# Making the first projections of a layer during the last expert periods of the layer ahead

## The chip, the cores and the metric

The kernel runs on one core of a Trainium2 chip. The metric is the device time of one execution in microseconds. The profile is of one execution of the same program, and its times below count from the first instruction of that execution.

## The reference, cut to what matters

Two blocks of two layers each run one after the other on 256 latent tokens, with 256 context tokens beside them, all in float32. A layer is a mixer followed by an expert stage:

```
xl = norm(hl) * (1 + scale) + shift          # latent tokens
xc = the same for the context tokens
y  = mixer(xl, xc) @ w_out;  hl += gate * y
hl += gate * experts(hl)                     # per token 8 heads x 16 experts of 16384
```

The mixers are: layer 0, a recurrent cell beside a differential attention; layer 1, windowed attention with key and value heads shared (16 query heads, 4 key and value heads); layer 2, attention through a latent vector (`zq` 384 wide, `zkv` 320 wide, both projections of the normalized tile); layer 3, pooling on latent tokens alone. From layer 1 on the context tokens only give keys and values. In layer 1 their projection is `kv` (512 wide: 256 of keys, 256 of values); in layer 2 it is `zkv` (256 that are normalized, 64 that hold the rotary part), and the context is an input of its own, `ctx_2`.

The expert stage projects a token to 16 vectors of 128, scores each against 128 keys, picks 16 experts for a head, gathers the two rows `u` and `v` of each (1024 float32 each), and sums `gate * gelu(u.x) * v`.

## The kernel before, in words

Tokens lie in four tiles of 128 partitions: tiles 0 and 1 are context (`CTX`), 2 and 3 latent (`LAT`). `H` holds the residual stream. The work of each engine is written out by hand, in order, with three step counters (one for each of TensorE, VectorE and ScalarE) on which the others wait.

A layer's **front** is its input and first projections. `front_input(t)` transposes the normalized tile `xn(l, t)` (8 transposes of 128x128), ScalarE or VectorE copy it from PSUM to `xT`, and `natural(l, name, (t,), ...)` multiplies it by a weight block (8 products of 128x128 by the block's width; each is two matmul instructions in the trace, a transposition is one). In layer 1 the front's order on TensorE is: `kv` of tiles 0 and 1, then for tiles 2 and 3 `kv`, `q0`, `q1`. In layer 2: `zkv` of tiles 0 and 1, then `zkv`, `zq` of tiles 2 and 3. In layer 3: `in0`, `in1` of tiles 2 and 3. Between them stand `take_beside()` calls, each one block of the modulation product for the next layer (2 MB of weights, 16 matmul instructions; every fourth also adds a bias, line 588, and ScalarE then copies and stores the group, `take_mods`). The rest of the twelve blocks stand in the attention loop, at the steps in `MODS_L1` (35 steps in layer 1).

Weights come in blocks, issued in a fixed order by SyncE (`block_list`, line 439) into five slots: 0 and 1 of a weight ring, `x0`, `x1` (which lies over two slots of the experts' ring) and `gates`. An issue waits until the slot's last block is used up, and the blocks behind it wait with it. `q0`, `zq`, `in1` and blocks in `x1` also wait for the sum of the third-last expert of the layer ahead.

An **expert period** (a unit) is 16 experts of one head for one tile. `POOL` issues a gather of 128 rows of 8 KB (1 MB) for each (line 494) into a ring of 8 slots, VectorE makes the dot product (line 2056), ScalarE the weight and a diagonal matrix (lines 1282 to 1286), TensorE the sum in PSUM (line 1007, two products 512 wide, four matmul instructions in the trace), and that sum frees the slot for the gather eight further on. Layer 0 has 32 periods, the others 16. Beside the 16 experts of a period, at the places in `PE_BESIDE` and `ACT_BESIDE`, stand the query products and scores of the period three ahead (`query`, `take`), and on VectorE the top-k of the period two ahead. In the last 16 periods, here called tail 0 to tail 15, no query is left for tails 13 to 15 and no top-k for tails 14 and 15. VectorE puts the context's normalized tiles in `H` (`next_context`) by tail 5, and from tail 12 on the norm of tile 2 and its next input (`end_of_layer(l, 2)`); that of tile 3 comes after the last sum.

## Time and profile before

| | |
|---|---|
| median of 3 runs | 4391.81 us (4379.93 to 4396.69) |
| the profiled execution | 4388.36 us, span 4386.6 us |
| TensorE busy | 3685.0 us (84%), mean granted clock 0.955 |
| VectorE busy | 2780.4 us (63%) |
| ScalarE busy | 1619.3 us (37%) |
| GpSimd busy | 1404.8 us (32%) |
| DMA | 1569.57 MB, mean 358 GB/s, 75.7% of it the experts' gathers |

The busy shares are means over stages with different limits. The expert stages run from 507 to 1827 us (layer 0), 2084 to 2723 (layer 1), 3006 to 3612 (layer 2) and 3777 to the end (layer 3); between them lie the mixers.

### The profile page before, as it was taken

What the parts mean: (1) busy time and instruction counts of PE and PEld (TensorE: products, weight loads), DVE (VectorE), ACT (ScalarE), POOL (GpSimd) and SP (SyncE); (2) the same over time, 40 slices, a digit from 0 to 9 for tenths busy, and PEclk for the clock granted to TensorE, in tenths of its full rate; (3) what the DMA queues carried; (4) which work ended last, traced back from release to release, by engine and by line L of the source; (5) the groups of instructions that cost most, each with busy time, mean ns of one, the idle gap of its engine ahead of it and who ended that gap; (6) DMA issues with size and microseconds to landing.
All of it is one profiled execution on the core that took longest, in us unless ns stands there. A gap on an engine that the chain in (4) does not pass through costs nothing.

```text
span 4386.6 us, 42868 instructions
## 1 busy us (share of the span) xinstructions
PE 3685.0 (84%) x11886; PEld 1734.8 (40%) x11886; DVE 2780.4 (63%) x7000; ACT 1619.3 (37%) x4854; POOL 1404.8 (32%) x1337
## 2 busy tenths in 40 slices
PE   5997988888888888898888888888888878888886
PEld 2444433344333333355333333453333324333332
DVE  3227766677776677446766675357667755766775
ACT  0123234444444344232444443124444431444443
POOL 0000243444443444201444442014434431434342
PEclk7988999999999999998999999999999999999999
DMA  6335699999999999863999999649999995999997
GB/s 248 135 136 202 262 421 421 421 419 413 413 419 419 416 414 407 330 274 146 421 421 421 420 410 374 238 183 421 421 421 420 411 390 207 411 421 421 421 411 333
DMA packets 207216, 1569.57 MB, mean 358 GB/s; under 512 B 23072, under 2 KB 23200, under 8 KB 30592
## 3 DMA queue, kind: packets, MB, share of 16 engines
q0 software_dynamic: 191952, 1370.57, 75.7%
q1 hardware_dynamic: 14832, 196.06, 11.4%
q8 instruction: 94, 1.54, 0.1%
q14 instruction: 146, 1.20, 0.1%
q10 hardware_dynamic: 192, 0.20, 0.0%
HBM read 1565.50 MB, written 1.25 MB: 357 GB/s over the span
## 4 chain that ended last, share of the span: by engine, by line
DMA 47%; PE 26%; DVE 9%; ACT 5%; issue 3%; DVEq 1%; POOL 1%; ACTq 0%; POOLq 0%
DMA arena<-uv,idx 46%; PE banks L1007 13%; PE banks L547 5%; DVE arena L2056 5%; PE banks L665 2%; ACT diag L1286 1%; PE banks L580 1%; ACT wgt L1284 1%; ACT gel L1282 1%; ACT L1282 1%; ACT L1070 1%; PE banks L840 1%; DMA weight_ring<-weights 1%; PE banks L561 1%; POOL arena L494 1%
## 5 line engine op out<-in xcount | busy, mean ns | idle before, releaser
L1007 PE MATMUL banks<-arena,diag 128*128 128x512 f32 x5120 | 2514.6, 627 | 547.7 <-ACT diag L1286 542.6
L494 POOL DMA_INDIRECT arena<-uv,idx x1280 | 1375.6, 1075 | 2313.3 <-PE banks L1007 1799.0
L2056 DVE CUSTOM_DVE_ANT_0 arena<-arena 128x1024 f32<-128x1024 f32 x1280 | 1566.8, 1225 | 854.0 <-DMA arena<-uv,idx 836.4
L1007 PEld LDWEIGHTS banks<-arena,diag 128*128 128x128 f32 x5120 | 926.7, 196 | 1982.2 <-ACT diag L1286 1205.8
L1282 ACT ACTIVATE gel<-dot 128x1 f32<-128x1 f32 x1280 | 258.5, 202 | 1674.1 <-DVE dot L2056 1672.7
L1286 ACT ACTIVATE diag<-consts_sb,wgt 128x128 f32<-128x128 f32 x1280 | 514.0, 402 | 92.2 <-issue 5.2
L1284 ACT ACTIVATE wgt<-gel,gate 128x1 f32<-128x1 f32 x1280 | 376.8, 294 | 90.4 <-issue 3.2
L547 PE MATMUL banks<-weight_ring,arena 128*128 128x512 f32 (+2 forms) x876 | 369.2, 580 | 5.3 <-DVE hidden_sb L1565 1.8
L547 PEld LDWEIGHTS banks<-weight_ring,arena 128*128 128x128 f32 x876 | 165.6, 191 | 198.4 <-issue 185.9
L471 POOL DMA_DIRECT2D row_ring<-mods x34 | 18.6, 556 | 598.3 <-DMA mods<-diag 256.2
L665 PEld LDWEIGHTS banks<-arena,weight_ring 128*128 128x128 f32 x1408 | 170.3, 192 | 39.7 <-issue 39.5
L665 PE MATMUL banks<-arena,weight_ring 128*128 128x128 f32 x1408 | 170.7, 275 | 0.0
L665 PEld LDWEIGHTS banks<-arena 128*128 128x128 f32 x1152 | 143.8, 199 | 31.3 <-issue 28.5
L665 PE MATMUL banks<-arena 128*128 128x128 f32 x1152 | 144.9, 282 | 3.3 <-ACT arena L1042 1.7
L580 PE MATMUL banks<-weight_ring,silu_cond 128*32 128x512 f32 x640 | 91.8, 699 | 37.7 <-DMA weight_ring<-weights 37.7
L1042 ACT COPY arena<-banks 128x512 f32<-128x512 f32 (+1 forms) x49 | 26.4, 573 | 223.0 <-PE banks L645 120.6
L2056 DVE DVE_READ_ACCUMULATOR2_ANT dot<- 128x1 f32 x1280 | 105.8, 83 | 0.0
L1282 ACT ACT_TABLE_LOAD x76 | 97.5, 1283 | 1.3
L1070 ACT ACT_TABLE_LOAD x73 | 93.7, 1283 | 1.3
L1536 DVE COPY arena<-banks 128x512 f32<-128x512 f32 (+3 forms) x43 | 25.5, 619 | 78.3 <-PE banks L533 58.1
L675 PEld LDWEIGHTS banks<-arena 128*128 128x128 f32 x320 | 48.9, 194 | 51.5 <-issue 31.2
L1561 DVE TENSOR_TENSOR arena<-banks,row_ring 128x512 f32<-128x512 f32 (+1 forms) x30 | 25.9, 864 | 68.2 <-PE banks L547 55.6
(252 smaller groups left out, 2353.2 us busy)
## 6 DMA issues: line engine op xcount, KB each, us to landing
weight_ring<-weights SPq DMA_DIRECT2D x67, 2048.0 KB, 7.9
arena<-weights SPq DMA_DIRECT2D x18, 2048.0 KB, 11.5
arena<-uv,idx POOLq DMA_INDIRECT x1280
row_ring<-mods POOLq DMA_DIRECT2D x34, 512.0 KB, 14.1
row_ring<-gains POOLq DMA_DIRECT2D x18, 512.0 KB, 13.8
arena<-keys SPq DMA_DIRECT2D x4, 1024.0 KB, 13.6
weight_ring<-weights SPq DMA_DIRECT2D x2, 1536.0 KB, 14.7
arena<-weights SPq DMA_DIRECT2D x3, 1024.0 KB, 9.9
```

What stands on the lines that cost most here:

```text
L494: pool.indirect_dma_start(out=ring[:, RING_SLOT[k], :], out_offset=None, in_=A[f"uv{l}"], in_offset=bass.IndirectOffsetOnAxis(ap=idx[:, UN ...
L547: ins = mm_(bank[:, b, 0:c1 - c0], src(kk, t), w[:, kk, c0:c1], start=kk == 0, stop=kk == k - 1)
L561: ins = mm_(bank[:, b, 0:ncols], w[:, kk, c * P:(c + 1) * P], src(kk), start=kk == 0, stop=kk == k - 1)
L580: ins = mm_(bank[32 * j:32 * j + 32, 7, :], cond, w[:, k2, j * 512:(j + 1) * 512], start=q == 0 and k2 == 0, stop=False, skip_group_check= ...
L665: ins = mm_(bank[:, b, 0:P], w[:, kk, c * P:(c + 1) * P], xT2[:, kk, i * P:(i + 1) * P], start=kk == 0, stop=kk == KC - 1)
L675: ins = mm_(bank[:, b, q * P:(q + 1) * P], qT[:, 2 * m + q, :], keys_sb[:, 2 * h + q, :], start=True, stop=True)
L1007: ins = mm_(bank[:, yb, :], diag[:, s, :], ring[:, s, D + hf * 512:D + hf * 512 + 512], start=first, stop=last, skip_group_check=True)
L1070: AF(ex[:, :], cv[:, :], ACT.Exp, bias=neg[:, :], accum_out=es[:, :]).then_inc(sems["act"], done("act", ("exps", *u)))
L1282: AF(gel[:, s:s + 1], dot[:, s:s + 1], ACT.Gelu)
L1284: AF(wgt[:, s:s + 1], gel[:, s:s + 1], ACT.Copy, scale=gate[:, n, j:j + 1])
L1286: AF(diag[:, s, :], ident, ACT.Copy, scale=wgt[:, s:s + 1]).then_inc(sems["act"], done("act", ("diag", k)))
L2056: sig(V.tensor_tensor_reduce(out=ring[:, s, 0:D], in0=ring[:, s, 0:D], in1=xnat_of(u[0], u[1]), scale=1.0, scalar=0.0, op0=ALU.mult, op1=A ...
```

## The change

The context's projections of layers 1 and 2 and the first product of tile 2 in layers 1, 2 and 3 are made during the last seven expert periods of the layer ahead. A one-tile buffer in a part of `XNAT` that is free then holds the transposed input. The context results are kept in `H[:, t, 0:512]`, from where the attention reads them; layer 2's norm of the context latents moves with them (`context_latents`).

```
+XAHEAD = (None, XNAT + D, XNAT + 2 * D, XNAT + 2 * D)
+AHEAD_NAME = (None, "kv", "zkv", "in0")
-PE_BESIDE = {0: (2, 5, 8, 12, 13), None: (2, 7, 11, 13, 14)}
-ACT_BESIDE = {0: (3, 6, 9, 13, 14), None: (4, 9, 12, 13, 15)}
+PE_BESIDE = {0: (2, 5, 8, 12, 13), None: (2, 6, 9, 12, 14)}
+ACT_BESIDE = {0: (3, 6, 9, 13, 14), None: (4, 8, 10, 13, 15)}
-    out += block("x0", 1, "kv") + block(0, 1, "q0") + mods(2, 0, 1) + block("x1", 1, "q1")
+    out += block("x0", 1, "kv") + block(0, 1, "q0") + block("x1", 1, "q1") + mods(2, 0, 1)
-MODS_L1 = (1, 4, 8, 12, 16, 20)
+MODS_L1 = (0, 2, 5, 8, 11, 14, 17, 20)
...
 # GpSimd: the load of ctx2 into H waits longer
-                    pool.wait_ge(*after("mm", 1, "xT", 1, 1))
+                    pool.wait_ge(*after("mm", 1, "O", 31))
...
 # TensorE, front of layer 1
-                    for t in CTX:
-                        front_input(t)
-                    for t in CTX:
-                        front_ready(t)
-                        natural(1, "kv", (t,), xs, KC, 512, last=False)
+                    for name in ("q0", "q1"):
+                        natural(1, name, LAT[:1], xs, KC, 512, last=False)
                     take_beside()
-                    for t in LAT:
-                        front_input(t)
-                    for t in LAT:
-                        front_ready(t)
-                        natural(1, "kv", (t,), xs, KC, 512, last=t == 3)
-                        if t == 3:
-                            take_beside()
-                        for name in ("q0", "q1"):
-                            natural(1, name, (t,), xs, KC, 512, last=t == 3)
-                            take_beside()
+                    front_input(3)
+                    front_ready(3)
+                    for name in ("kv", "q0", "q1"):
+                        natural(1, name, LAT[1:], xs, KC, 512)
+                        take_beside()
...
 # TensorE, front of layer 2
+                    natural(2, "zq", LAT[:1], xs, KC, 384, last=False)
                     take_beside()
+                    front_input(3)
+                    front_ready(3)
+                    natural(2, "zkv", LAT[1:], xs, KC, 320)
+                    natural(2, "zq", LAT[1:], xs, KC, 384)
+                    for _ in range(4):
+                        take_beside()
...
 # TensorE, front of layer 3
+                    natural(3, "in1", LAT[:1], xs, KC, 512, last=False)
+                    front_input(3)
+                    front_ready(3)
+                    for j in range(2):
+                        natural(3, f"in{j}", LAT[1:], xs, KC, 512)
...
 # TensorE, beside the experts (ScalarE has the copies in the same places)
+                def ahead_input(m, t):
+                    pe.wait_ge(*after("xn", m, t))
+                    for half in range(2):
+                        b = new_bank(m, "xT", t, half)
+                        for k in range(4):
+                            ins = nc.tensor.transpose(...)
+                        ins.then_inc(sems["pe"], done("pe", ("mm", m, "xT", t, half)))
+                        yield
+                def ahead_product(m, t):
+                    name = AHEAD_NAME[m]
+                    width = 320 if m == 2 else 512
+                    n, w = weights((m, name), KC)
+                    pe.wait_ge(*after("ev", m, "xT", t, 0))
+                    pe.wait_ge(*after("ev", m, "xT", t, 1))
+                    b = new_bank(m, name, t, 0)
+                    for kk in range(KC):
+                        ins = mm_(bank[:, b, 0:width], xahead(m)[:, kk, :], w[:, kk, :], ...)
+                        if kk == 3:
+                            yield
+                    ins.then_inc(sems["pe"], done("pe", ("mm", m, name, t, 0)))
+                    yield
...
+                    tail = n - len(units) + 16
+                    if l < 2 and 9 <= tail <= 12:
+                        t = (tail - 9) // 2
+                        beside = chain(beside, ahead_input(l + 1, t) if tail % 2 else ahead_product(l + 1, t))
+                    if l < 3 and tail == 14:
+                        beside = chain(wait_turns(3), ahead_input(l + 1, 2))
+                    if l < 3 and tail == 15:
+                        beside = ahead_product(l + 1, 2)
...
 # ScalarE, layer 1: the group of modulations moves behind the copies of v; layer 3: a wait for the last sum
-                    for t in tiles:
-                        if t == 3:
-                            take_mods(6)
+                    for t in LAT:
...
+                    take_mods(6)
...
 # VectorE, in tails 12 to 15 of layer 1
+            def context_latents():
+                _, mg = row(2, "mlag", 0)
+                for t in CTX:
+                    c = H[:, t, 0:256]
+                    dve.wait_ge(*after("ev", 2, "zkv", t, 0))
+                    V.tensor_copy(H[:, t, 320:384], H[:, t, 256:320])
+                    V.tensor_copy(H[:, t, 384:448], H[:, t, 256:320])
+                    sig(dve.drain(), ("kr", t))
+                    squares(c, H[:, t, 512:768], small[:, 32 + t:33 + t])
+                    yield
+                    rsqrt(small[:, 32 + t:33 + t], 1.0 / 256, EPS)
+                    yield
+                    dve.drain()
+                    sig(V.scalar_tensor_tensor(out=c, in0=c, scalar=small[:, 32 + t:33 + t], in1=mg[:, 384:640], ...), ("zkv_n", t))
+                    yield
```

## Rows read from the trace of the kernel before

**Rows 1.** The page's part 4: the chain that ended last, share by engine.

```profile
DMA 47%; PE 26%; DVE 9%; ACT 5%; issue 3%; DVEq 1%; POOL 1%; ACTq 0%; POOLq 0%
```

**Rows 2.** Windows of 5 us: width, busy (count) by engine, clock, DMA share, GB/s.

```profile
1685.00:1690.00 5.00, 4.77 (x23) 3.03 (x23) 4.62 (x12) 2.44 (x9) 3.61 (x2) 1.00 0.90 339
1690.00:1695.00 5.00, 5.00 (x13) 2.28 (x12) 4.47 (x10) 2.13 (x8) 2.83 (x2) 1.00 1.00 367
1695.00:1700.00 5.00, 3.97 (x13) 1.73 (x12) 3.30 (x11) 1.84 (x6) 3.32 (x4) 1.00 0.95 336
...
1790.00:1795.00 5.00, 4.00 (x9) 1.38 (x9) 2.46 (x4) 1.80 (x6) 1.91 (x3) 1.00 1.01 421
```

**Rows 3.** Timeline of TensorE about the end of layer 0's experts.

```profile
1672.73 1.95 PE L665 MATMUL banks<-arena,weight_ring 128*128 128x128 f32 x16
...
1824.69 1.98 PE L1007 MATMUL banks<-arena,diag 128*128 128x512 f32 x4 [0.47 <-ACT diag L1286]
...
1830.28 13.90 PE L547 MATMUL banks<-arena 128*128 128x512 f32 x32
```

**Rows 4.** The chain in order of time, layer 1's front: start, us, what.

```profile
1863.72 7.44 DMA weight_ring<-weights
...
1873.18 7.78 DMA weight_ring<-weights
...
1899.79 1.85 PE banks L580 x16
...
1905.19 1.18 PE banks L820 x4
```

**Rows 5.** Timeline of SyncE: weight issues at the end of layers 0, 1, 2.

```profile
1821.84 0.80 SPq L439 DMA_DIRECT2D weight_ring<-weights  x2
...
2718.08 0.33 SPq L439 DMA_DIRECT2D weight_ring<-weights  x1
...
3607.48 0.33 SPq L439 DMA_DIRECT2D weight_ring<-weights  x1
```

**Rows 6.** The page's part 6: median us from issue to landing.

```profile
weight_ring<-weights SPq DMA_DIRECT2D x67, 2048.0 KB, 7.9
```

**Rows 7.** Timeline of VectorE: last step of tile 3's input, layers 1, 2, 3.

```profile
1835.06 1.23 DVE L1419 TENSOR_TENSOR arena<-arena,row_ring 128x1024 f32<-128x1024 f32 x1
...
2732.84 1.23 DVE L1419 TENSOR_TENSOR arena<-arena,row_ring 128x1024 f32<-128x1024 f32 x1
...
3624.50 1.23 DVE L1419 TENSOR_TENSOR arena<-arena,row_ring 128x1024 f32<-128x1024 f32 x1
```

**Rows 8.** Windows as in 2: the attention loop of layer 1.

```profile
1905.20:2003.60 98.40, 90.48 (x625) 64.64 (x626) 55.56 (x194) 49.79 (x133) 0.00 (x0) 0.84 0.42 168
```

**Rows 9.** Timeline of TensorE, layer 2's front.

```profile
2725.63 8.85 PE L547 MATMUL banks<-weight_ring,arena 128*128 128x320 f32 x32 [0.96 <-DVE hidden_sb L1567]
...
2749.62 9.73 PE L547 MATMUL banks<-weight_ring,arena 128*128 128x320 f32 x32
...
2768.98 3.64 PE L580 MATMUL banks<-weight_ring,silu_cond 128*32 128x512 f32 x16 [5.04 <-DMA weight_ring<-weights]
...
2774.95 1.92 PE L580 MATMUL banks<-arena,silu_cond 128*32 128x512 f32 x16 [0.81 <-ACT diag L1053]
```

**Rows 10.** Timeline of TensorE, layer 3's front.

```profile
3615.03 13.97 PE L547 MATMUL banks<-weight_ring,arena 128*128 128x512 f32 x32 [1.83 <-DVE hidden_sb L1565]
3628.84 1.04 PE L533 MATMUL banks<-consts_sb,arena 128*128 128x128 f32 x8
3630.71 13.97 PE L547 MATMUL banks<-weight_ring,arena 128*128 128x512 f32 x32 [0.83 <-ACT arena L1042]
```

**Rows 11.** The chain in order of time, last period of layer 0's experts.

```profile
1787.27 15.24 DMA arena<-uv,idx
```

**Rows 12.** Windows of 2 us, as in 2, in layer 1's attention loop.

```profile
1962.00:1964.00 2.00, 1.05 (x4) 0.23 (x4) 1.70 (x7) 0.71 (x2) 0.00 (x0) 1.00 0.98 410
...
1966.00:1968.00 2.00, 2.00 (x12) 2.00 (x12) 0.32 (x2) 1.45 (x4) 0.00 (x0) 0.50 1.12 474
```

More of the change, by code:

```diff
@@ L394, in program, with xahead, wait_turns @@
         xT2 = v3(XT2, KC, 2 * P)
+        def xahead(l):
+            return v3(XAHEAD[l], KC, P)
+        def wait_turns(n):
+            for _ in range(n):
+                yield
         qT = v3(QT, 4, P)
@@ L1105, in _ @@
                 if l < 3:
-                    for t in tiles:
-                        front_input(t, 2 if l and t < 3 else 1)
+                    for t in tiles if l == 0 else (3,):
+                        front_input(t, 1)
                 if l == 2:
@@ L1286, in expert_weight, with ahead_input, ahead_product @@
                     AF(diag[:, s, :], ident, ACT.Copy, scale=wgt[:, s:s + 1]).then_inc(sems["act"], done("act", ("diag", k)))
+                def ahead_input(m, t):
+                    for half in range(2):
+                        copy_T((m, "xT"), t, xahead(m)[:, 4 * half:4 * half + 4, :], half)
+                        yield
+                def ahead_product(m, t):
+                    yield
+                    b = b_(m, AHEAD_NAME[m], t, 0)
+                    c = 320 if m == 2 else 512
+                    ev(a.copy(H[:, t, 0:c], bank[:, b, 0:c]), m, AHEAD_NAME[m], t, 0)
+                    yield
                 units = units_of(l)
@@ L1299, in _ @@
                         beside = take(units[n + 3])
+                    tail = n - len(units) + 16
+                    if l < 2 and 9 <= tail <= 12:
+                        t = (tail - 9) // 2
+                        beside = chain(beside, ahead_input(l + 1, t) if tail % 2 else ahead_product(l + 1, t))
+                    if l < 3 and tail == 14:
+                        beside = chain(wait_turns(3), ahead_input(l + 1, 2))
                     if n == 0:
@@ L2112, in _ @@
                     run(beside)
-                    if (n in (10, 13) and l == 0) or n == len(units) - 11 or tail == 14:
+                    if (n in (10, 13) and l == 0) or n == len(units) - 11 or tail == (15 if l == 1 else 14):
                         run(between)
```

65 lines of the change are left out of this document (29 added, 36 removed).

## The prediction

> **What bounds the kernel now.** I read the chain that ended last first. It goes through DMA for 47% of the span and through TensorE for 26% [rows 1], so there is no single limit: the next thing to read is which stage has which. In windows of 5 us a quiet stretch of an expert stage moves 421 GB/s with the DMA engines full [rows 2], the most that any expert window shows. A gather is 1.049 MB, so a period of 16 needs 39.9 us of DMA. TensorE's part of the same period comes from its timeline: 32 matmul instructions 512 wide took 13.90 us, 0.434 each [rows 3], so the 64 of a period's sums take 27.8 us and its query products about 4.4 us (two groups of 1.95 and some 0.5 for the scores) [rows 3]: 32.2 us. The ring is thus bound by DMA with 7.7 us of TensorE to spare in a period, 12.1 where no query is left. The fronts are the opposite. After the last sum (end 1826.7) TensorE works almost without a break to the last modulation block before layer 1's attention (1901.6) [rows 3, 4]. There the bound is TensorE with short waits for weights: the two DMA pieces of the chain, 7.44 and 7.78 us, lie mostly behind a product, since a block is issued only when the last one in its slot is used up [rows 4]. So the change takes work from where TensorE is the bound to where DMA is. What it is worth must be read from each front.
>
> **Layer 1's front.** It loses the transpositions of tiles 0, 1 and 2 (1.04 each [rows 10]), the `kv` product of those three tiles (6.95 each [rows 3]) and two of six modulation blocks (1.85 each [rows 4]). Laid out anew: `q0` is issued at 1821.84 [rows 5] and with the median landing of 7.9 [rows 6] is there at 1829.7. `q0` and `q1` of tile 2 take 13.9, to 1843.6 (`q1`, issued right behind and moved ahead of the modulation block, lands about 5 us after `q0`, in time). Then one block (1.85): 1845.5. Tile 3's input was ready at 1836.3 [rows 7], so it does not hold. Transposition 1.04 and 0.83 until it is copied [rows 10]: 1847.4. Then `kv` 6.95, block 1.85, `q0` 6.95, block, `q1` 6.95, block: 1873.8. The blocks all lie in slot 1, each issued when the last is used up; 7.8 to land [rows 4] against a product of 6.95 that covers it leaves about 0.9 a block, twice: 1875.6, and 0.9 for the bias: 1876.5. Before it was 1901.6, so 25.1 us less. Two things take some back. ScalarE now copies and stores the modulation group (some 1.8 us) just before its six copies of the transposed keys and queries, on which the first scores wait: 1.4. And two more blocks stand in the attention loop, 3.7 us; TensorE is busy 90.5 of 98.4 us there [rows 8], so little of it is free, but the one at step 0 stands where the loop fills: 3.0. Bounds for these two together: 0 (both in gaps) to 5.5. **Layer 1: 20.7 us less.** The later load of `ctx2` costs nothing: nothing but the gathers, which wait longer anyway, stands behind it on GpSimd, and VectorE asks for it a period later. The context copies in the attention are read from `H` instead, at no price.
>
> **Layer 2's front.** It loses `zkv` of tiles 0 to 2 (32 instructions for two tiles took 8.85, so 4.4 a tile [rows 9]), three transpositions, and on VectorE two of six norms. But tile 3's input is ready only at 2734.1 [rows 7], and the work that covered that wait is gone. `zq` is issued at 2718.1 [rows 5], 1.5 MB, there by about 2725; 5.3 us (the rest of 9.7 for `zkv` and `zq` together [rows 9]), a block to about 2732.4, then TensorE waits to 2734.1, 1.04 and 0.83 more, and 9.7 for tile 3: about 2746. `zkv`'s slot is then free at 2740.6 instead of 2754.2, 13 to 14 us earlier, and behind it the blocks come one after another as they did: in the trace the fourth starts at 2768.98 after 5.04 idle, and the fifth ends at 2776.9 [rows 9]. All of that chain of landings moves with the slot. The fourth block took 3.64 instead of 1.9, and was held by the load of the fifth, issued with it; now that one is issued 2 us behind. I take 15 (bounds 12 and 18). **Layer 2: 15 us less.**
>
> **Layer 3's front.** `in1` is issued at 3607.5 [rows 5], there at 3615.4; 7.0 us to 3622.4. Tile 3's input is ready at 3625.7 [rows 7]: with the product gone TensorE now waits 3.3 us. Then 1.04, 0.83 and the two products 13.97: 3641.6 instead of 3644.7 [rows 10]. **Layer 3: 3 us less.** Of 8 us that it gives away, 5 are lost to VectorE's chain. The wait that ScalarE gets here is for a sum long made.
>
> **The expert periods.** Added on TensorE in the layers 0 and 1: in tails 9 to 12, twice 1.04 and 6.95 (layer 0: 16.0 us), twice 1.04 and 4.4 (layer 1: 10.9); in tails 14 and 15 8.0, 5.4 and 8.0 us in layers 0, 1, 2. Together 48.3 us. The cover is the ring: eight gathers are 19.9 us of DMA, and of that a gather spends 15.24 between issue and landing [rows 11], of which 2.5 are its own transfer: the rest, some 12 us less what a lone gather needs to start, it waits behind others, and the engines may be late by that before DMA runs dry. A half product (3.5 us) between two sums fits, and is made good at 0.75 us an expert. In tails 14 and 15 nothing else competes: nothing. In tails 9 to 12 it is not so clean. There the ring already ran dry once: 339, 367 and 336 GB/s in three windows of tail 12 [rows 2] lose 2.6 us, where VectorE has the top-k, the residual and the norm of tile 2, and TensorE then worked through its backlog (5.00 of 5). A half product put behind such a backlog costs up to its length. ScalarE, too, waits at expert 15 for the second half product before it can copy it, and with it the next period's first weight. Bounds: 0, and 26.9 if all of tails 9 to 12 shows. Only tail 12 of two layers is near dry, and about one half product in each (3.5 and 2.2) falls there: **5 us more**. VectorE's norm of the context latents (two times about 4 us) lies in tails 13 to 15 of layer 1, where it is idle half of the time: nothing. With that cover gone it would be 8. The moved places of the queries change nothing that I can find: each still has ScalarE's copy two experts before its use.
>
> **Sum.** 20.7 + 15 + 3 - 5 = 33.7 us less than the profiled execution's 4388.4: 4354.7. That execution was 3.4 under the median of the runs, so I say **4358**.
>
> **The clock.** In layer 1's attention the granted clock fell from 1.00 to 0.50, that is from 2.4 to 1.2 GHz, after TensorE had been busy only 1.05 of 2 us [rows 12], and the loop's mean is 0.84 [rows 8]. The new waits in the fronts of layers 2 and 3 are of that size. The price from rows: the products behind a fall run at half speed, as the fourth block of layer 2 did (3.64 for 1.92 [rows 9]); if it takes half of layer 3's two products and of layer 2's 9.7, that is 12 us more. If on the other hand the denser blocks keep the loop of layer 1 at full clock, its 16 points of clock on 98.4 us are worth up to 15, say 10. The Trainium skill, in "TensorE: Matmul & The Clock Gate", section "What's actually happening", states that the throttled state is the default and that activity releases it; by that rule the new waits speak against this change, and the sum would be 12 us worse. The trace has waits of 1.8 us at both fronts (layers 1 and 3) with the clock kept, so I leave it out of the sum.
>
> **Rivals and chances.**
> 1. My forecast, 4348 to 4368: 0.55.
> 2. The ring has no room in tails 9 to 12: all 26.9 shows instead of 5, 4380. For it: the dry windows [rows 2]. Against it: 7.7 us spare in each period. 0.13.
> 3. The products are not hidden at all, tails 14 and 15 included: 48.3 for nothing against 38.7 gained, 4401, slower than before. It decides at 38.7 us lost of 48.3; beyond that the ring at a half clock would be needed for over 0.5%. Against it: in the last period TensorE is busy 4.0 of 5 us [rows 2]. 0.04.
> 4. The clock falls in the new waits (12 more): 4370. 0.12.
> 5. The clock holds in layer 1's loop (10 less): 4348 or under. 0.08.
> 6. The weights bound the fronts: with the cover gone, each block of modulation waits for its landing in full, some 8 us more in layer 1 and 6 in layer 2: 4372. 0.08.
>
> The 80% range takes in cases 4, 5 and 6 and most of 2: 4340 to 4378. A measurement of this kernel can tell about 0.5% (22 us) from no change, so faster means under 4370: most of case 1, all of 5, half of 4 and a third of 6. That is 0.74; slower by over 0.5% is 0.03; the rest 0.23.
>
> **What would show it.** In the profile after: `kv`, `zkv` and `in0` products beside sums at line 1007 of tails 10, 12 and 15; layer 1's attention starting about 24 us sooner after the last sum than the 78.5 us of before (1826.7 to 1905.2 [rows 3, 4]); in layer 2 the first `uqn` product about 15 sooner; in layer 3 only 3 sooner, with an idle TensorE that waits for VectorE; expert stages of layers 0 and 1 a few us longer, of layer 2 equal. The forecast is wrong if the windows of tails 9 to 12 show DMA well under 421 GB/s for more than 5 us a layer, or the clock is near 0.5 in the new fronts.

## The result, and the profile after

| | before | after |
|---|---|---|
| median of the runs | 4389.59 us (4 runs, 4379.93 to 4396.69) | 4344.36 us (4 runs, 4342.51 to 4351.19) |
| ratio of the runs | | 0.9904, 95% interval 0.9891 to 0.9917 |
| the profiled execution | 4388.36 us | 4343.52 us |
| TensorE busy, mean clock | 3685.0 us, 0.955 | 3659.4 us, 0.958 |

By the ratio the change made the kernel 42 us faster (36 to 48 by the interval), 1.0% of its time; 34 were forecast. 4344 lies within the stated range of 4340 to 4378, but below the 4348 to 4368 of the forecast's own case, where rival 5 had its place. Two pairs of profiles of the same two programs give the stages. For each stage the table has the time between two products of TensorE: from the first to the last sum of an expert stage, from there to the next layer's first product behind its front (the scores in layer 1, `uqn` in layer 2, the pooling in layer 3), through layer 1's attention loop, and the rest of the mixer.

| us | before | before, again | after | after, again | forecast |
|---|---|---|---|---|---|
| start to first sum | 506.8 | 519.4 | 512.6 | 512.9 | 0 |
| experts 0 | 1319.9 | 1319.8 | 1319.5 | 1319.3 | } |
| experts 1 | 660.5 | 660.5 | 661.8 | 661.8 | } +5 |
| experts 2 | 662.2 | 662.0 | 662.7 | 662.2 | } |
| experts 3 | 654.1 | 653.1 | 653.9 | 653.7 | 0 |
| front of layer 1 | 78.5 | 78.7 | 54.5 | 57.2 | -23.7 |
| its attention loop | 96.4 | 96.3 | 90.6 | 88.4 | +3.0 |
| its rest | 60.9 | 60.8 | 58.4 | 60.0 | 0 |
| front of layer 2 | 58.1 | 57.9 | 42.4 | 46.9 | -15 |
| its rest | 169.0 | 169.1 | 168.5 | 168.8 | 0 |
| front of layer 3 | 33.3 | 33.3 | 30.3 | 33.4 | -3 |
| its rest | 72.7 | 72.7 | 72.6 | 72.7 | 0 |
| first sum to last sum | 3865.6 | 3864.3 | 3815.3 | 3824.4 | -33.7 |

The first row is untouched by the change and yet varies by 12.6 us from one execution to the next, about as much as the whole times of before's two profiles differ (11.3), which is why I read effects of a few us from the stages.

Two figures given ahead of the prediction are to be read otherwise. By the first sum the expert stages of before start at 506.8, 2062.4, 2950.1 and 3718.3 us (the later ones not at 2084, 3006 and 3777). And 75.7% is the share of the 16 DMA engines' time that the gathers' queue took; of the bytes it moved 1371 of 1570 MB, 87%. The loop of before ends at 2001.6, so the window of [rows 8] and the loop lengths in the expectations (98.4, 92.7) count some 2 us of what follows it.

The page's part 4 of after, against [rows 1]: three points of the chain have gone from DMA to TensorE and ScalarE.

```profile
DMA 44%; PE 28%; DVE 9%; ACT 6%; issue 3%; DVEq 1%; POOL 1%; ACTq 0%; POOLq 0%; SPq 0%
```

The timeline of TensorE in after, last period of layer 0's experts and on into layer 1's front (start, us, what, and in brackets the idle time before and what ended it). Line 1008 is the sum, line 1032 the new product, in two halves, line 557 `natural`:

```profile
1797.89 1.98 PE L1008 MATMUL banks<-arena,diag 128*128 128x512 f32 x4 [0.50 <-ACT diag L1323]
1799.71 3.60 PE L1032 MATMUL banks<-arena 128*128 128x512 f32 x8
1803.14 7.03 PE L1008 MATMUL banks<-arena,diag 128*128 128x512 f32 x16
1810.01 3.60 PE L1032 MATMUL banks<-arena 128*128 128x512 f32 x8
1813.44 8.80 PE L1008 MATMUL banks<-arena,diag 128*128 128x512 f32 x20
1822.74 1.98 PE L1008 MATMUL banks<-arena,diag 128*128 128x512 f32 x4 [0.50 <-ACT diag L1323]
...
1830.12 1.98 PE L1008 MATMUL banks<-arena,diag 128*128 128x512 f32 x4 [0.47 <-ACT diag L1323]
```

This is the whole mechanism in a few lines. A sum (four instructions, 1.98) is normally followed by 0.5 us of idleness. After each half product of 3.60 TensorE runs sums back to back: four, then five. By 1822.74 the 0.5 us gap is back, so the delay is paid off, and the last sum is on time. DMA stayed full meanwhile. Windows of after in the same columns as [rows 2]. The first two lie just behind the products of tail 10, the next two in tail 12, with its top-k and the norm of tile 2, the two after them where tail 13 begins:

```profile
1630.00:1635.00 5.00, 5.00 (x13) 2.06 (x12) 3.21 (x9) 1.73 (x6) 0.80 (x1) 1.00 0.99 360
1635.00:1640.00 5.00, 5.00 (x14) 2.20 (x12) 4.36 (x16) 2.33 (x9) 3.26 (x3) 1.00 0.92 329
...
1695.00:1700.00 5.00, 5.00 (x15) 2.33 (x14) 4.60 (x10) 1.77 (x7) 1.87 (x2) 1.00 0.86 323
1700.00:1705.00 5.00, 5.00 (x16) 2.34 (x15) 3.65 (x10) 2.77 (x10) 3.01 (x3) 1.00 0.99 375
...
1715.00:1720.00 5.00, 5.00 (x12) 2.01 (x11) 4.44 (x16) 3.59 (x13) 1.89 (x2) 1.00 0.94 383
1720.00:1725.00 5.00, 5.00 (x13) 2.26 (x12) 4.56 (x15) 1.96 (x7) 3.44 (x4) 1.00 0.93 341
...
1800.00:1805.00 5.00, 5.00 (x13) 2.23 (x12) 2.47 (x4) 1.83 (x7) 0.94 (x1) 1.00 1.01 421
```

In tail 12 the rates 323, 375 and then 406 cost DMA 1.9 us, where the 339, 367 and 336 of before [rows 2] cost 2.6: the new pieces did not deepen that dip, which stands where VectorE is busiest (up to 4.6 of 5 us). But there is a new one. From 1630 to 1645, right behind the two halves of tail 10 (they start at 1622.56 and 1629.43), the rates are 360, 329 and 365, which cost 2.5 us; before has 419 to 424 there. In the second execution of after it comes again (354 and 338 from 1632.3 to 1642.3), and the one of tail 12 does not. Over tails 9 to 12 of layer 0 (four windows of 39.87 us, counted back from the last sum) DMA loses 5.3 and 3.3 us against 421 GB/s in after's two executions and 4.5 in both of before, so what the new pieces take in one place is made up in another, and the stage is not longer.

The chain of after through layer 1's front, in order of time, as in [rows 4]:

```profile
1827.28 7.69 DMA weight_ring<-weights
...
1861.74 7.97 DMA weight_ring<-weights
```

`q0` landed 2.9 us after the last sum ended (1832.1), and two blocks of modulation idled TensorE for 1.01 and 0.81, the rest of their 7.97 and 7.77 us of landing lying behind a product.

The timeline of TensorE in after, fronts of layers 2 and 3, as in [rows 9, 10]; the last sums ended at 2697.5 and 3571.1:

```profile
2699.17 5.43 PE L557 MATMUL banks<-weight_ring,arena 128*128 128x384 f32 x16 [1.70 <-DMA weight_ring<-weights]
...
2708.30 1.09 PE L543 MATMUL banks<-consts_sb,arena 128*128 128x128 f32 x8 [1.85 <-DVE arena L1476]
2710.23 9.71 PE L557 MATMUL banks<-weight_ring,arena 128*128 128x320 f32 x32 [0.83 <-ACT arena L1078]
...
2728.86 3.27 PE L590 MATMUL banks<-weight_ring,silu_cond 128*32 128x512 f32 x16 [3.60 <-DMA weight_ring<-weights]
...
3573.92 8.83 PE L557 MATMUL banks<-weight_ring,arena 128*128 128x512 f32 x16 [2.85 <-DMA weight_ring<-weights]
3584.50 1.09 PE L543 MATMUL banks<-consts_sb,arena 128*128 128x128 f32 x8 [1.76 <-DVE arena L1476]
3586.43 13.97 PE L557 MATMUL banks<-weight_ring,arena 128*128 128x512 f32 x32 [0.83 <-ACT arena L1078]
```

Both fronts now wait for VectorE (line 1476, the last step of tile 3's input, line 1419 before) where a product stood. In layer 3 the clock had already fallen once, behind the wait of 2.85 us: the windows from 3574 to 3578 have it at 0.68 and 0.50, and `in1` took 8.83 us, where it took 7.13 in the second execution behind a wait of 3.01. It cost nothing there, since the product ends ahead of VectorE all the same. And the loop of layer 1, with the stretch in which its clock is down, against [rows 8]:

```profile
1945.00:1950.00 5.00, 3.18 (x24) 2.31 (x23) 3.19 (x11) 2.74 (x9) 0.00 (x0) 1.00 0.94 384
1950.00:1955.00 5.00, 5.00 (x20) 3.47 (x19) 2.32 (x9) 2.60 (x8) 0.00 (x0) 0.50 0.99 424
1955.00:1960.00 5.00, 4.73 (x30) 3.74 (x28) 3.34 (x12) 2.51 (x6) 0.00 (x0) 0.82 0.50 208
...
1886.60:1977.20 90.60, 81.33 (x642) 55.17 (x643) 54.05 (x189) 48.92 (x131) 0.53 (x1) 0.96 0.59 239
```

The mean clock rose from 0.84 to 0.96. This is the one place where the sign of a term was wrong.

### The profile page after: what moved, and what is told of

Same layout as the page of the kernel before. It is cut to its first block, busy times and chain, and to the rows that moved or that the text cites. A ratio compares the mean times of both kernels' runs of the same rounds, so it can differ in the third digit from the quotient of the medians.

```text
span 4341.7 us, 42866 instructions
## 1 busy us (share of the span) xinstructions
PE 3659.4 (84%) x11886; PEld 1730.5 (40%) x11886; DVE 2777.5 (64%) x6996; ACT 1620.4 (37%) x4856; POOL 1442.2 (33%) x1337
## 4 chain that ended last, share of the span: by engine, by line
DMA 44%; PE 28%; DVE 9%; ACT 6%; issue 3%; DVEq 1%; POOL 1%; ACTq 0%; POOLq 0%; SPq 0%
DMA arena<-uv,idx 43%; PE banks L1008 16%; DVE arena L2126 4%; PE banks L557 4%; PE banks L675 2%; ACT diag L1323 1%; DMA weight_ring<-weights 1%; PE banks L590 1%; ACT wgt L1321 1%; ACT L1319 1%; ACT L1106 1%; POOL arena L504 1%; ACT gel L1319 1%; PE banks L847 1%; PE banks L571 1%
## 5 line engine op out<-in xcount | busy, mean ns | idle before, releaser
L504 POOL DMA_INDIRECT arena<-uv,idx x1280 | 1413.1, 1104 | 2167.9 <-PE banks L1008 1761.8
L557 PE MATMUL banks<-weight_ring,arena 128*128 128x512 f32 (+2 forms) x812 | 350.6, 591 | 10.8 <-DMA weight_ring<-weights 7.5
L557 PEld LDWEIGHTS banks<-weight_ring,arena 128*128 128x128 f32 x812 | 153.8, 191 | 198.7 <-issue 178.8
L675 PEld LDWEIGHTS banks<-arena,weight_ring 128*128 128x128 f32 x1408 | 171.5, 193 | 40.2 <-issue 39.9
L675 PE MATMUL banks<-arena,weight_ring 128*128 128x128 f32 x1408 | 171.8, 276 | 0.0
```

The costliest lines, as they stand in the source:

```text
L504: pool.indirect_dma_start(out=ring[:, RING_SLOT[k], :], out_offset=None, in_=A[f"uv{l}"], in_offset=bass.IndirectOffsetOnAxis(ap=idx[:, UN ...
L557: ins = mm_(bank[:, b, 0:c1 - c0], src(kk, t), w[:, kk, c0:c1], start=kk == 0, stop=kk == k - 1)
L675: ins = mm_(bank[:, b, 0:P], w[:, kk, c * P:(c + 1) * P], xT2[:, kk, i * P:(i + 1) * P], start=kk == 0, stop=kk == KC - 1)
```

## The experiments

### Both kernels once more

The same programs, profiled again.

> The kernel before, unchanged, for a second profile. Two theories of why layer 1's attention loop took 98.4 us before and 92.7 after, though two modulation blocks more stand in it: (a) each execution differs in how long the clock stays at half speed after ScalarE's copy and store of the last modulation group (32 us before, 8 us after), so a second profile of the same kernel may give anything from 88 to 98 us for the loop; (b) the order of the blocks before decides it, so this profile shows the long stretch at half clock and 97 to 99 us again. The time as before, 4380 to 4397.

> The kernel after, unchanged, for a second profile and a tighter ratio: 0.989 to 0.991. (a) the loop of layer 1 takes anything from 90 to 100 us; (b) 92 to 93.5 us again, with the half clock for less than 12 us. The expert stages last as long as before within 2 us each under both.

Before: 4399.69 us (one run). After: 4351.53 us median, ratio 0.9909 (0.9882 to 0.9937). In before, the loop and its half clock came again as (b) had it; in after the loop took 88.4 us and had no half clock at all, which is outside (b) (90 to 91.5 us by this count). Before repeats to 0.2 us in all three fronts and in the loop; after does not: its fronts took 57.2, 46.9 and 33.4 us instead of 54.5, 42.4 and 30.3. TensorE's timeline of the second execution of after, at the first product of layer 1's front and in the fronts of layers 2 and 3:

```profile
1835.33 10.04 PE L557 MATMUL banks<-weight_ring,arena 128*128 128x512 f32 x16 [3.05 <-DMA weight_ring<-weights]
...
2710.47 1.09 PE L543 MATMUL banks<-consts_sb,arena 128*128 128x128 f32 x8 [1.88 <-DVE arena L1476]
2712.39 12.70 PE L557 MATMUL banks<-weight_ring,arena 128*128 128x320 f32 x32 [0.83 <-ACT arena L1078]
...
3590.98 1.09 PE L543 MATMUL banks<-consts_sb,arena 128*128 128x128 f32 x8 [3.30 <-DVE arena L1476]
3592.91 17.04 PE L557 MATMUL banks<-weight_ring,arena 128*128 128x512 f32 x32 [0.83 <-ACT arena L1078]
```

and windows of 2 us of the same execution:

```profile
3588.00:3590.00 2.00, 0.00 (x0) 0.00 (x0) 1.70 (x3) 0.00 (x0) 1.09 (x2) 1.00 0.11 23
...
3594.00:3596.00 2.00, 2.00 (x4) 0.91 (x3) 0.00 (x0) 0.00 (x0) 0.00 (x0) 0.50 1.01 344
```

The products that took 7.13, 9.71 and 13.97 us took 10.04, 12.70 and 17.04; in layer 3 the window behind the wait for VectorE has the clock at 0.50, that is 1.2 GHz. In layer 1 the wait ahead of `q0` (3.05, against 2.92 in the first execution) is longer than the one that before has in this place, 1.84 us for VectorE, behind which two `kv` products took their 13.90 us [rows 3]. So rival 4 is real but does not come at the same place every time: a wait of 1.85 us kept the clock in one execution and one of 1.88 was followed by the slow product in the other. It costs up to 3 us a front, and in layer 3 that is exactly the gain of the change.

### The attention loop: who breaks the clock

In before the clock was at 0.50 for about 30 us of the loop, in both executions. The windows of before, second execution:

```profile
1974.00:1979.00 5.00, 3.17 (x18) 2.31 (x18) 2.96 (x10) 2.28 (x7) 0.00 (x0) 0.85 0.97 413
1979.00:1984.00 5.00, 5.00 (x23) 4.05 (x22) 2.41 (x9) 2.72 (x8) 0.00 (x0) 0.50 0.97 413
...
1999.00:2004.00 5.00, 5.00 (x26) 4.88 (x26) 2.91 (x9) 2.30 (x6) 0.00 (x0) 0.50 0.02 3
```

Just before the fall, in the first execution of before, TensorE's timeline has a gap:

```profile
1964.88 1.08 PE L830 MATMUL banks<-consts_sb,arena 128*128 128x128 f32 x4 [1.82 <-ACT small L1213]
```

It falls at step 21, where ScalarE stops to copy and store a group of modulations (`take_mods(8)`: 0.58 us for the copy, 1.38 for issuing four stores), one step behind the last block. Moved behind the loop, it stops nobody:

```
-                        if step == MODS_L1[-1] + 1:
-                            take_mods(8)
...
                 if l in (1, 2):
                     for t in LAT:
                         copy_T((l, "mT"), t, ...)
+                    if l == 1:
+                        take_mods(8)
```

In the kernel before:

> The kernel before, with the same move alone. If the pause of ScalarE drops the clock: loop 98.4 to about 86 to 89 us, no half clock in it, 4378 to 4382, ratio 0.9975 to 0.9985. If the clock falls anyway: loop 96 us or more, ratio 0.9990 to 1.0005.

and in the kernel after:

> The kernel after, with ScalarE's copy and store of the last modulation group of layer 1 moved from step 21 of the attention loop to behind the loop. Nothing then holds ScalarE, and through it TensorE, before step 22. If that pause is what drops the clock, there is no window under 1.0 in the loop, the loop takes 88 to 90 us instead of 92.7, and the ratio to before is 0.9885 to 0.9900. If the clock falls from the thinner work after the last block itself, there is still a stretch at 0.5 and the loop takes 91 us or more.

In before the loop went from 96.4 to 86.6 us; in after from 90.6 or 88.4 to 87.5. The whole loops, in windows, of before with the late store and then of after with it:

```profile
1914.60:2001.20 86.60, 75.86 (x610) 53.28 (x611) 53.53 (x190) 47.82 (x130) 0.00 (x0) 0.98 0.47 190
```

```profile
1890.60:1978.10 87.50, 78.15 (x642) 52.74 (x643) 53.87 (x189) 48.21 (x130) 0.53 (x1) 1.00 0.61 247
```

The mean clock over the loop is 0.98 and 1.00, against 0.84 [rows 8]. The long stretch at 0.50 is gone with the store, but not every half clock: in before with the late store it falls once for 3.4 us, behind the pause of 1.58 us that the group of modulations in the middle of the loop makes (`take_mods(7)`):

```profile
1930.60:1934.60 4.00, 3.48 (x18) 3.51 (x18) 1.15 (x6) 1.82 (x7) 0.00 (x0) 0.57 0.08 32
```

The long fall stands behind the store in both profiles of before and is missing in the one without the store, so I take the store at step 21 as its trigger. It does not make one every time. All eight profiles of after and its variants that keep the store have the same pause of 1.82 or 1.83 us; in five the clock then stood at 0.50 for some 7 us (loops of 90.5 and 90.6 us), in three it did not fall (88.3 to 88.7). In whole times the evidence is weaker: before with the late store has 4383.86 us, ratio 0.9991 (0.9978 to 1.0003), so between 10 us gained and 1 lost where its profile, first sum to last, gained 9.6; the ratio expected was 0.9975 to 0.9985, and this one fits the rival's 0.9990 to 1.0005 as well. After with it has 4348.25, ratio 0.9912 (0.9891 to 0.9934), no different from after and above the 0.9885 to 0.9900 expected.

With the store out of the way on both sides the two more blocks can be priced: 87.5 against 86.6, so 0.9 us. The clock is not quite equal, for the 86.6 hold the short fall; a fall of the same length made the loop of another kernel below 89.2 instead of 87.5, and with that 1.7 taken off the blocks cost 2.6. So by this estimate they cost 0.9 to 2.6, where I had said 3.0.

### Only the places of the query products

```
-PE_BESIDE = {0: (2, 5, 8, 12, 13), None: (2, 6, 9, 12, 14)}
-ACT_BESIDE = {0: (3, 6, 9, 13, 14), None: (4, 8, 10, 13, 15)}
+PE_BESIDE = {0: (2, 5, 8, 12, 13), None: (2, 7, 11, 13, 14)}
+ACT_BESIDE = {0: (3, 6, 9, 13, 14), None: (4, 9, 12, 13, 15)}
```

> The kernel after with the places beside the experts (where queries and the new pieces stand on TensorE and ScalarE) put back to those of before. In the profile after, the first four periods of the expert stages of layers 1, 2 and 3 took 3 us less than before and the last eight 3 us more, in layer 3 too, where nothing was added. Theory: the new places do both, and cost nothing in sum, so here the stages show neither shift and last as long within 1.5 us, ratio 0.989 to 0.992. Rival: the shifts are of another cause (they stay), or the new places are worth some us (ratio 0.992 or more).

4349.39 us, ratio 0.9912 (0.9886 to 0.9938). The four expert stages: 1320.3, 662.2, 661.6, 654.0, within 1.1 us of after. The shifts of 3 us that the expectation starts from I can't find in the starts of the dot products: the first four periods of layer 1 took 171.8 us in before, 171.7 in after and 171.6 here, the last eight 325.2, 326.6 and 327.1. The moved places give and cost nothing.

### Layer 3's part undone

```
-                    if l < 3 and tail == 14:
+                    if l < 2 and tail == 14:
...
-                    if l < 3 and tail == 15:
+                    if l < 2 and tail == 15:
```

(on TensorE and ScalarE, and the front of layer 3 as in before).

> The kernel after with the part for layer 3 alone undone (transposition and in0 product of tile 2 back in its front). Theory of the prediction: 3 us of its 8 were gained, as VectorE's chain to the input of tile 3 bounds the front: front 33.3 instead of 30.3 us from last sum to the first pooling product, layer 2's expert stage unchanged, time 3 us more than after (ratio 0.990 to 0.992). Rival: 8.0 us of product and transposition in tails 14 and 15 were not free, so that undoing them shortens layer 2's experts by more than 1 us and the time does not rise.

4352.25 us, ratio 0.9915 (0.9889 to 0.9942). The front of layer 3 took 32.3 us, against 30.3, 33.4, 31.8 and 31.9 in the four executions told of so far that have the part. The expert stage of layer 2 took 662.3 against 662.7 and 662.2: its product in tail 15 cost nothing, and giving it back saves nothing. Layer 3's part is worth 2 us where the clock holds and nothing, or minus 1, where it falls. By whole times (4352.25 against 4344.36 and 4351.53) it can't be told.

### How much room the ring has

Each of the new products is made twice, the first result being overwritten by the second, so that a piece between two sums has 16 instructions instead of 8:

```
-                    for kk in range(KC):
+                    for n2 in range(2 * KC):
+                        kk = n2 % KC
                         ins = mm_(bank[:, b, 0:width], xahead(m)[:, kk, :], w[:, kk, :], start=kk == 0, ...)
-                        if kk == 3:
+                        if n2 == KC - 1:
                             yield
```

> The kernel after, with each product that was moved into the expert periods made twice into the same bank (the first result is overwritten): seven 7 or 4.4 us products more on TensorE, 43.6 us in all, in two pieces of 7 us instead of 3.5. If the ring has room as the profile after suggests (the moved 48 us cost 0 to 1 us), the doubled ones cost little in tails 14 and 15 and some in tails 10 and 12 of layers 0 and 1: 3 to 10 us more than after. If the forecast's 5 us were there and hidden in noise: over 15 us more. If they stood on the path in full: 44 us more, and slower than after by 1%.

4361.97 us, ratio 0.9934 (0.9912 to 0.9956). That is 10 to 18 us more than after, where 3 to 10 were expected. By the stages against after: layer 0's experts +8.9, layer 1's +1.4, layer 2's +2.5. This points to the length of a piece and not to the sum of the work: three products in pieces of 7.03 cost 8.9 (3.0 each) and the single one of layer 2 cost 2.5, while the three of layer 1, 320 wide and in pieces of about 4.4, cost 1.4 together, though they are more work than layer 2's one. It is not shown outright: the experiment doubles both, and the same work in twice as many short pieces was not run. TensorE in this kernel, last period of layer 0:

```profile
1807.32 7.03 PE L1033 MATMUL banks<-arena 128*128 128x512 f32 x16
1814.18 7.03 PE L1008 MATMUL banks<-arena,diag 128*128 128x512 f32 x16
1821.05 7.03 PE L1033 MATMUL banks<-arena 128*128 128x512 f32 x16
1827.92 15.61 PE L1008 MATMUL banks<-arena,diag 128*128 128x512 f32 x36
```

and GpSimd's timeline at the gathers held up by the two pieces (they otherwise wait about 1.6 us):

```profile
1816.34 1.27 POOL L504 DMA_INDIRECT arena<-uv,idx  x1 [7.65 <-PE banks L1008]
...
1830.07 0.94 POOL L504 DMA_INDIRECT arena<-uv,idx  x1 [7.49 <-PE banks L1008]
```

Here the sums never catch up: after the second piece nine of them follow back to back (x36) to the end of the stage, where in after the gap was back by 1822.74. This prices rival 2. Its mechanism exists, but pieces of 3.60 us cost nothing here, and pieces of 7.03 do.

### The first block of the next front earlier

`q0`, `zq` and `in1` wait for the sum of the third-last expert, and each lands after the last sum. Waiting three sums less, and one sum less:

```
-                    sp.wait_ge(*after("sum", slot_at(units_of(l - 1)[-1], TOPK - 3)))
+                    sp.wait_ge(*after("sum", slot_at(units_of(l - 1)[-1], TOPK - (3 if where == "x1" else 6))))
```

> The kernel after, with the first weight block of each front (q0, zq, in1) issued three sums earlier, when the last gathers of the layer are already issued. TensorE waits 2.92, 1.70 and 2.85 us for it after the last sum. In layer 1 the wait should go: 2.9 us less. In layers 2 and 3 the front then waits longer for tile 3's input from VectorE, so 0. Sum 3 us less than after, ratio 0.9885 to 0.9905. Rival: the block takes turns with the last gathers and delays the last sum by up to 5 us each: 0 to 8 us more than after.

4380.1 us, ratio 0.9985 (0.9972 to 0.9998): nearly the whole gain of the change is gone. Neither the forecast (3 us less) nor the rival (0 to 8 more) had this. The expert stages took 1328.3, 670.3 and 669.7 us, 8.8, 8.5 and 7.0 more than in after. VectorE's last dot products in layer 0:

```profile
1830.53 1.22 DVE L2126 CUSTOM_DVE_ANT_0 arena<-arena 128x1024 f32<-128x1024 f32 x1 [3.08 <-DMA arena<-uv,idx]
...
1838.12 1.23 DVE L2126 CUSTOM_DVE_ANT_0 arena<-arena 128x1024 f32<-128x1024 f32 x1 [6.36 <-DMA arena<-uv,idx]
```

The block was issued at 1823.94, while the last gathers were still in flight, and the last of them landed 7.0 us later than in after, counted from the first sum; 2.1 MB at 421 GB/s are 5.0 us. The rest of the 8.8 is the clock: behind a wait of 4.99 us the last sum took 3.78 instead of 1.98. Nor are the 7.0 the price of this block alone: the two blocks behind it were issued at 1830.59 and 1830.96, once the third-last sum was made, as in after, but here the last gather was still on its way until 1838.1 and shared the engines with them. How the delay divides among the three is not shown. The Trainium skill, in "DMA: Bandwidth & Descriptors", section "Issuing engines are not separate DMA queues", says that transfers of different issuers run on the same 16 engines and interleave. This case agrees: weights that SyncE issued delayed gathers that GpSimd had issued.

With `TOPK - 4` in place of `TOPK - 6`:

> The kernel after, with the first weight block of each front issued one sum earlier (with the third sum ahead of the last instead of the second). Three sums earlier made each of the three expert stages 7 to 9 us longer, as the last two gathers landed late. Theory: the block only does harm while gathers are still being fetched; the last lands some 3 us after this issue, about when the block's own transfer starts, so the stages grow by under 1.5 us and layer 1's front loses up to 2.5 us of its wait: ratio 0.989 to 0.991. Rival: any issue before the last landing costs a full block (5 us or more a stage, ratio 0.993 or more).

4349.19 us, ratio 0.9906 (0.9889 to 0.9922). Now the expert stages are as in after (1318.8, 661.7, 662.2) and the front of layer 1 is 2.8 us shorter, 51.7, because `q0` is waited for 0.57 us instead of 2.92. But the fronts of layers 2 and 3 took 46.3 and 33.6, 3.9 and 3.3 more than in after's first execution and as much as in its second (46.9 and 33.4). TensorE there:

```profile
2707.61 1.97 PE L543 MATMUL banks<-consts_sb,arena 128*128 128x128 f32 x8 [3.81 <-DVE arena L1476]
2710.41 11.53 PE L557 MATMUL banks<-weight_ring,arena 128*128 128x320 f32 x32 [0.83 <-issue]
...
3587.13 1.97 PE L543 MATMUL banks<-consts_sb,arena 128*128 128x128 f32 x8 [5.73 <-DVE arena L1476]
3589.93 16.36 PE L557 MATMUL banks<-weight_ring,arena 128*128 128x512 f32 x32 [0.83 <-issue]
```

There the first product is not what ends last, VectorE's chain is. An earlier block only turns a wait ahead of the product into a longer one behind it (3.81 and 5.73 us), and behind that the clock is down: the transpositions took 1.97 instead of 1.09. Since after itself is as slow in one execution of two, this run does not show that the longer wait made it worse.

### Constant products in the waits

A helper `warm(n, b)` multiplies the identity by constants into a bank that is overwritten afterwards: two such products ahead of layer 2's last input, three ahead of and three behind layer 3's `in1`. No output depends on them.

```
+                def warm(n, b):
+                    for _ in range(n):
+                        mm_(bank[:, b, :], ident, consts[:, 0:512], start=True, stop=True, skip_group_check=True)
...
                     natural(2, "zq", LAT[:1], xs, KC, 384, last=False)
                     take_beside()
+                    warm(2, b)
                     front_input(3)
...
+                    warm(3, 7)
                     natural(3, "in1", LAT[:1], xs, KC, 512, last=False)
+                    warm(3, 7)
                     front_input(3)
```

> The kernel after, with products of constants (their result is overwritten) on TensorE in its new waits: two 512 wide before tile 3's transposition in layer 2, three before in1 and three before tile 3's transposition in layer 3. In the second profile of the kernel after, the 9.7 us products of tile 3 in layer 2 took 12.7 and the 14.0 us of layer 3 took 17.0, behind waits of 1.9 and 3.3 us, at a granted clock of 0.50; in the first they did not. Theory: the wait drops the clock, in some executions. Then here both fronts are at their best every time: 42 to 43.5 us and 30.3 to 30.8 us from last sum to first product of the next part, and no window at 0.5 between tile 2's products and the end of tile 3's. Rival: the fall is of another cause; then a window of 0.5 shows here too. Time 0 to 5 us less than after, which its runs hardly tell.

4348.46 us, ratio 0.9914 (0.9895 to 0.9932). TensorE in both fronts:

```profile
2705.83 1.98 PE L797 MATMUL banks<-consts_sb 128*128 128x512 f32 x4
2707.66 1.08 PE L543 MATMUL banks<-consts_sb,arena 128*128 128x128 f32 x8
2709.56 9.71 PE L557 MATMUL banks<-weight_ring,arena 128*128 128x320 f32 x32 [0.83 <-ACT arena L1089]
...
3580.69 2.74 PE L797 MATMUL banks<-consts_sb 128*128 128x512 f32 x6
3584.18 1.09 PE L543 MATMUL banks<-consts_sb,arena 128*128 128x128 f32 x8 [0.75 <-DVE arena L1487]
3586.10 13.97 PE L557 MATMUL banks<-weight_ring,arena 128*128 128x512 f32 x32 [0.83 <-ACT arena L1089]
```

The fronts took 43.1 and 30.3 us: the shorter times of after's two executions, with 9.71 and 13.97 for the products. In windows of 2 us the clock is 1.00 throughout, from tile 2's products to behind the first of tile 3's. That supports the reading that the idle wait is what costs the clock. But after itself reached the same times in one execution of two, and the kernel with doubled products, which has no fillers, had 42.9 and 30.3 us, so two profiles with fillers (this and the next) do not prove that they hold it.

Together with the late store:

> The kernel after with the late store of layer 1's last modulation group and the constant products in the waits, both. Late store alone took 2 to 3 us off the loop of layer 1 (87.5 against 90.6 and 88.4); with the fronts at 42.4 and 30.3 us, the time from the first expert sum to the last should be 3812 to 3816 us (after: 3815.3 and 3824.4), ratio 0.9885 to 0.9905.

4345.39 us, ratio 0.9901 (0.9884 to 0.9917); loop 89.2, fronts 54.0, 43.5 and 30.4; first sum to last 3814.8. The fillers alone had 3814.8 too: here the late store added nothing, for the clock fell for 3.4 us behind the pause of 1.59 us at the middle group. Among the variants this has the lowest ratio, 0.9901, but its interval and that of after (0.9891 to 0.9917) overlap almost wholly. No version beats the change measurably. What the fillers and the late store would at best remove is the three slow products of after's second execution, 9 us.

## Why the prediction was right

- **Layer 1's front** (forecast 23.7 us less until the first scores, that is 25.1 less 1.4): 24.0 in the first pair of profiles, 21.5 in the second, where `q0`'s product ran 2.9 us longer. The order of the new front came out as laid out: `q0` 2.9 us behind the last sum (forecast 3.0), two waits of about 0.9 for modulation (1.01 and 0.81), no wait for tile 3's input.
- **The attention loop** (forecast 3.0 us more for two more blocks): 5.8 and 7.9 less. This step failed, in sign. The blocks themselves cost 0.9 to 2.6, not far from it; what the sum put at nothing was the clock. The loop of before lost some 10 us to a clock that stood at 0.50 for 30 us, and after loses some 2 or nothing. I had this as rival 5 with a chance of 0.08 and "say 10" for its size; the size was close, the chance far too low. The low clock stood in the rows [rows 8, 12], and I did not ask what triggered it. The late store points to the trigger in before. Why the same store, in after likewise one step behind the last block, is followed by only 7 us at 0.50 or none is not settled: the two kernels differ there in the number and the places of the blocks and in where `v` is read, and I tried no version that changes one of these alone. The loop's 6 to 8 us came in both pairs, but for the forecast they are luck.
- **Layer 2's front** (forecast 15 less): 15.7 and 11.0. Tile 3's products start 12.8 us after the last sum (forecast 13.1), and the fourth block of modulation, at 2728.86, comes 31.4 us after it where it came 46.1 after it in before [rows 9]. The prediction had the 3.64 us of this block in before as the work of the next load, and in its part on the clock as a fall. It was the clock: the windows from 2768 to 2774 have it at 0.50 to 0.55 behind the wait of 5.04 us, and in after the block took 3.27, at 0.55 and 0.60 behind 3.60 us. The lower figure of the second pair is the clock behind the wait.
- **Layer 3's front** (forecast 3 less): 3.0, and in the second pair nothing. That VectorE's chain eats 5 of the 8 us was right. The wait was 1.8 us and not 3.3, since `in1` took 8.83 where I had 7.0; that moves the idle time, not the end. In the second execution it was 3.3, and behind it the clock fell.
- **The expert stages** (forecast 5 more, bounds 0 and 26.9): 1.2 in the first pair (-0.4, +1.3, +0.5, -0.2), 1.6 in the second (-0.5, +1.3, +0.2, +0.6). The 48 us of moved products are all but free. The argument from the ring's slack held; the 5 us for tail 12 (3.5 and 2.2 make 5.7) were too careful, for the dip in DMA there did not grow, and the new one behind tail 10 did not lengthen the stage. The +1.3 of layer 1, the same in both pairs, lies in its tail 13 (39.8 us from first dot product to the next period's before, 41.7 and 41.9 after), where VectorE has the norm of the context latents that the prediction put at nothing; its cause was not tested. The most that a window of 5 us shows is up to 429 GB/s and not 421, which is the steady rate. The doubled products show how near the edge lies: with pieces twice as long the same stages lose 12.8 us more.
- **Sum**: -33.7 forecast, -50.3 and -39.9 measured between first and last sum, and 42 (36 to 48) by whole times. The forecast of 4358 is 14 us above the median. In the first pair it is the loop (8.8 us between +3.0 and -5.8), the expert stages (4) and the rest of layer 1 (2.5) that came out better; in the second pair the loop's 10.9 are in part taken back by the clock in the three fronts, and the sum is only 6 off. So the mechanisms of fronts and experts were right, and the sum is as near as it is because the clock gave in one place and took in others.
- **Rivals**: 2 (no room in the ring) and 3 (nothing hidden) are refuted by the stage times. 6 (weights bound the fronts) shows only in the waits that were counted. 4 (clock falls in the new waits) happens in some executions, for up to 3 us in each of three fronts, where I had 12 in two. 5 happened. The 0.74 for faster is more than its parts add up to: 0.55, 0.08, 0.06 and 0.03 make 0.72.
- **The signs of being wrong**: both came up, and neither told. DMA is well under 421 GB/s in five windows of tails 10 to 12 of layer 0, but before has three such in tail 12 alone; what DMA lost had to be compared with before. The clock was near 0.5 in a new front in both executions.

The moved places of the queries, costed at nothing, cost nothing. The rest of layer 1 is 0.8 to 2.5 us shorter, and its clock differs between the two kernels there too; I did not follow it further.

## What to carry to other kernels

Where a DMA-bound loop has slack on TensorE, work from a front that is bound by TensorE can be put between its steps almost for nothing, as long as each piece is short against the ring's lead (here 3.6 us was free and 7.0 cost 2.5 to 3 us a product); look at whether the normal gap between steps returns before the stage ends. Emptying a front uncovers what lay behind the products: ask which chain of another engine is next, and what the new wait does to the clock. A transfer brought forward into the last steps of such a loop can cost more than its bytes, because the loop's end hangs on its last transfer, and one that is late meets the transfers that are due behind it.

## What the hardware showed that I had not expected

- A pause of TensorE of 1.82 us, made by a store on another engine, was followed by some 30 us at half clock (before, both executions), though the windows show TensorE busy 5.00 of 5 us. Without the store the loop was 9.8 us shorter. The same pause in eight profiles of after and its variants was followed by 7 us at half clock in five and by none in three. The Trainium skill, in "TensorE: Matmul & The Clock Gate", section "What's actually happening", has activity release the throttle; in these rows a TensorE shown as busy throughout stayed throttled, and what ended the episode is open.
- Nearly the same wait, 1.85 and 1.88 us at the same place of the same program, kept the clock once and lost it once; 2.85 us lost it and 3.01 kept it, in the same two executions. The price of such a wait is 0 to 3 us, by the execution.
- A load of 2.1 MB issued three sums early, with two more blocks behind it at their usual time, held up the last gathers of a stage so that it ended 7 to 9 us later, against 5.0 us for its bytes; issued one sum early it did not lengthen the stage.
- The front of layer 0, the same in all versions, took between 506.8 and 519.4 us.
